# Norms after the attention projection and after `down`: squares of two neighbouring chunks added on POOL, one ones-product per pair

## What is computed

```python
def rms_norm(x, g):
    xf = x.astype(jnp.float32)
    y = xf * lax.rsqrt(jnp.mean(xf * xf, axis=-1, keepdims=True) + RMS_EPS)
    return (y * g.astype(jnp.float32)).astype(x.dtype)

hp = modulate(rms_norm(xp, norm_g[l, 0]), sh1c, sc1c)
xp = xp + g1c * yp                                  # yp: attention @ w_o, or convolution @ w_pw2
hp = modulate(rms_norm(xp, norm_g[l, 1]), sh2c, sc2c)
xp = xp + g2c * (jnp.square(jax.nn.relu(hp @ w_up)) @ w_down)
```

## Time and profile before

| | us |
|---|---|
| three runs: median (lowest, highest) | 2685.6 (2671.91, 2939.64) |
| the profiled execution, its own time | 2670.14 |
| its span, slowest core (core 0) | 2668.6 |
| spans of the eight cores | 2657.3 to 2668.6 |
| mean granted TensorE clock of core 0 | 0.968 |

### The profile page before, as it was taken

How to read it: one execution, slowest core, us unless ns; L and a number is a source line. 1 busy time by engine, 2 the same in 40 slices (tenths; PEclk the granted TensorE clock), 3 DMA queues, 4 the chain that set the end, 5 groups by cost and what they waited for, 6 DMA issues and landing times.

```text
span 2668.6 us, 41955 instructions; the slowest of 8 cores (2657.3 to 2668.6 us)
## 1 busy us (share of the span) xinstructions
PE 2445.8 (92%) x14955; PEld 1077.7 (40%) x15184; DVE 1107.2 (41%) x1552; ACT 1051.0 (39%) x1563; POOL 336.8 (13%) x395
## 2 busy tenths in 40 slices
PE   2888889999999988999999888899999998899998
PEld 1322224444444443444443222344444454344443
DVE  1344444422325565323244554443232555632333
ACT  3455555301224466202254555551031445730224
POOL 1122220000001141000002322000000112200000
PEclk8999989999999989999999999899999998999999
DMA  9765533455543212555438444156664331233432
GB/s 208 149 87 69 71 57 62 78 99 100 99 76 68 54 29 48 102 101 98 79 73 155 56 56 56 20 76 101 99 101 72 61 60 31 32 48 50 55 54 95
DMA packets 133434, 205.99 MB, mean 77 GB/s; under 512 B 73136, under 2 KB 79280, under 8 KB 132464
## 3 DMA queue, kind: packets, MB, share of 16 engines
q0 software_dynamic: 109872, 161.70, 41.4%
q1 hardware_dynamic: 23360, 41.60, 4.7%
HBM read 322.89 MB, written 31.46 MB: 133 GB/s over the span
## 4 chain that ended last, share of the span: by engine, by line
PE 77%; DMA 6%; ACT 6%; issue 5%; DVE 5%; POOL 1%; DVEq 0%; ACTq 0%; POOLq 0%; SPq 0%
PE pp L654 23%; PE ps L654 19%; PE pp L677 7%; PE ps L884 4%; PE pp L1276 3%; DMA scr<-rpbp 3%; PE pp L1003 2%; PE ps L677 2%; PE pp L1404 2%; PE ps L1028 2%; PE ps L1276 2%; PE pp L1239 2%; PE ps L582 2%; DMA ring<-wall 2%; DVE scr L976 1%
## 5 line engine op out<-in xcount | busy, mean ns | idle before, releaser
L723 DVE TENSOR_TENSOR big<-big 128x512 bf16<-128x512 f32 x384 | 265.5, 692 | 415.8 <-ACT big L721 415.8
L654 PE MATMUL ps<-hTs,ring 128*128 128x512 bf16 x1488 | 339.0, 383 | 13.5 <-ACT hTs L632 8.5
L654 PE MATMUL pp<-hTs,ring 128*128 128x512 bf16 x1520 | 342.7, 380 | 1.9
L419 POOL DMA_DIRECT2D ring<-wall x140 | 99.1, 708 | 1712.7 <-PE pp L654 492.9
L654 PE MATMUL pp<-big,ring 128*128 128x512 bf16 x1362 | 304.9, 379 | 2.8 <-ACT big L721 1.2
L721 ACT ACTIVATE big<-ps 128x512 f32<-128x512 f32 x190 | 113.2, 596 | 472.5 <-PE ps L654 468.2
L575 ACT ACTIVATE scr<-xTs 128x512 bf16<-128x512 f32 x216 | 133.3, 626 | 318.8 <-DVE xTs L693 277.0
L693 DVE SCALAR_TENSOR_TENSOR xTs<-pp,mod,xTs 128x512 f32<-128x512 f32 x156 | 116.8, 750 | 330.2 <-PE pp L654 239.4
L976 DVE TENSOR_TENSOR scr<-pp,scr 128x768 f32<-128x768 f32 (+2 forms) x192 | 174.5, 910 | 143.1 <-PE pp L1009 69.3
L721 ACT ACTIVATE big<-pp 128x512 f32<-128x512 f32 x194 | 115.4, 596 | 296.7 <-PE pp L654 293.8
L654 PEld LDWEIGHTS ps<-hTs,ring 128*128 128x128 bf16 x1520 | 148.6, 98 | 192.3 <-issue 18.7
(11 more groups left out here) (120 smaller groups left out, 2689.8 us busy)
## 6 DMA issues: line engine op xcount, KB each, us to landing
ring<-wall POOLq DMA_DIRECT2D x140, 1024.0 KB, 11.2
vo<-big SPq DMA_DIRECT2D x48, 256.0 KB, 5.6
kTo<-big SPq DMA_DIRECT2D x48, 256.0 KB, 2.1
scr<-rpbp POOLq DMA_DIRECT2D x64, 128.0 KB, 3.6
xTs<-xT SPq DMA_DIRECT2D x3, 2048.0 KB, 19.8
yT<-scr SPq DMA_DIRECT2D x24, 256.0 KB, 2.2
scr<-big SPq DMA_DIRECT2D x64, 54.0 KB, 6.8
scr<-big POOLq DMA_DIRECT2D x64, 54.0 KB, 6.8
```

Of the source, the lines that this page charges most:

```text
L654: ins = e.matmul(ps[pi][:, :], lhsT=w[:, kc, fc * fw:(fc + 1) * fw], rhs=src[:, kc, t * 512:(t + 1) * 512], start=(kc == 0), stop=(kc == n ...
L723: P.op("dve", lambda e: e.tensor_tensor(out=hid[:, hc, t * 512:(t + 1) * 512], in0=ta[:, :], in1=ta[:, :], op=ALU.mult), reads=[ta_r], wri ...
```

## The change

`norm_begin` takes `pair`. With it, `norm_chunk` squares into an fp32 buffer of 128x512; for an even chunk it stops there. For an odd chunk POOL adds the two squares into a bf16 buffer, and the ones-product of this sum is deferred, with the lag that the odd chunk had. A tile has four ones-products instead of eight. It is set for the norm behind `o` and for the norm behind `down` if another layer follows; the final norm, the first one and those behind the convolution stay as they are.

```diff
+        ctx["np"] = 4 if pair else 8
+        ctx["sq"] = [scr.alloc(1024, BF16, f"sq{n}") for n in range(4 if pair else 6)]
+        if pair:
+            ctx["sqf"] = [scr.alloc(2048, F32, f"sqf{n}") for n in range(4)]
+            ctx["qf"] = 0
...
+        if ctx["np"] == 4:
+            sf, sf_r = ctx["sqf"][ctx["qf"] % 4]
+            ctx["qf"] += 1
+            P.op("act", lambda e: e.activation(out=sf[:, :], in_=xT[:, t, c, :], func=AF.Square),
+                 reads=[xT_r[c][t]], writes=[sf_r])
+            if c % 2 == 0:
+                ctx["half"] = (sf, sf_r, c, t)
+                return
+            s0, s0_r, c0, t0 = ctx["half"]
+            assert (c0, t0) == (c - 1, t)
+            sq, sq_r = ctx["sq"][ctx["q"] % 4]
+            ctx["q"] += 1
+            P.op("pool", lambda e: e.tensor_tensor(out=sq[:, :], in0=s0[:, :], in1=sf[:, :], op=ALU.add),
+                 reads=[s0_r, sf_r], writes=[sq_r])
...
-                                          start=(n == 0), stop=(n == 7)),
+                                          start=(n == 0), stop=(n == ctx["np"] - 1)),
...
-            if n == 7:
+            if n == ctx["np"] - 1:
...
-                nctx = norm_begin("mod", l + 1, 0) if l + 1 < DEPTH else norm_begin("final")
+                nctx = norm_begin("mod", l + 1, 0, pair=True) if l + 1 < DEPTH else norm_begin("final")
...
-        nctx = norm_begin("mod", l, 1)
+        nctx = norm_begin("mod", l, 1, pair=True)
```

More of the change, by code:

```diff
@@ L550, in build_program, with norm_begin @@
     ntiles = []
-    def norm_begin(kind, l=None, k=None, banks=(5, 6, 7)):
+    def norm_begin(kind, l=None, k=None, banks=(5, 6, 7), pair=False):
         flush_deferred()
@@ L555, in norm_begin @@
         ctx = {"kind": kind, "l": l, "k": k, "n": 0, "m": 0, "q": 0, "cnt": [0] * NT}
-        ctx["sq"] = [scr.alloc(1024, BF16, f"sq{n}") for n in range(6)]
+        ctx["np"] = 4 if pair else 8
[3 more added lines that the diff above has]
+            ctx["qf"] = 0
         ctx["rstd"] = [scr.alloc(2048, F32, f"rstd{n}") for n in range(2)]
@@ L572, in norm_chunk @@
         bk = ctx["bk"][t]
[L573 to L577, removed]
+        if ctx["np"] == 4:
[12 more added lines that the diff above has]
+                 reads=[s0_r, sf_r], writes=[sq_r])
+        else:
+            sq, sq_r = ctx["sq"][ctx["q"] % 6]
+            ctx["q"] += 1
+            P.op("act", lambda e: e.activation(out=sq[:, :], in_=xT[:, t, c, :],
+                                               func=AF.Square),
+                 reads=[xT_r[c][t]], writes=[sq_r])
         def part():
```

## The result

The changed kernel takes 1.0089 times the time before (95% interval 1.0059 to 1.0119), about 24 us more. In three of its five executions one die ran at a lower clock, so this goes by the other two, 2694.2 and 2699.0 us, and not by the median of 2744.19 us. Timed once more beside the experiments it took 1.0065 (1.0036 to 1.0093), about 17 us more. The forecast was 5 us more, 2676 us, with a range to 2697.

The account below looks back on a forecast made before the run. PE, busy for 92% of the span, was taken to bound the kernel. 13.0 us saved and 18.2 lost gave +5.2 on a profiled 2670.1, about 2675; it predicted 2676 us, range 2657 to 2697.

Parts of the forecast that it names:

- The price of the addition: On POOL, adding two fp32 128x512 tiles into bf16: 1.27 us taken, with bounds of 0.61 and 1.89.
- the places of the large stalls: PE waits for late sums: 2.03 us at product 11 of `o`; in `down` 0.9 at 17 and 21, 1.57 at 23.
- The saving of 13.0: On PE, five norms lose 12 ones-products each: 60 x 0.2165 = 13.0 us, 0.5% of the span.
- The rival of a slow addition: On POOL, the addition with bf16 output takes 1.89 us and nearly every pair stalls: 2703 us, chance 0.12.
- The rival that all is hidden: In the five norms, late products find unseen slack and all 13.0 us are kept: 2657 us, chance of this side 0.12.
- POOL's queue: Behind `o` and `down`, weight loads wait for the last sums; counted as hidden, uncovered up to 4 us at each of five places.
- A rival for late loads: At five places the loads become late behind the sums: 5 x 4 = 20 us, giving 2695 us, chance 0.05.
- 18.2: Microseconds PE was to lose in 17 places behind `o` and `down`, waiting for sums from POOL.
- small waits that were there before the change: In `o`, eight groups and eight products took 15.77 us instead of 15.56: a stall of 0.2 for each tile, which goes.
- +5.2: Net microseconds over five norms: +1.4 for each of two behind `o`, +0.8 for each of three behind `down`.
- the hand-overs: From square to product, ACT to POOL takes 0.15 us and POOL to PE 0.14; with the addition 1.56.

Follow-up runs that it names:

- early loads: The changed kernel with the two weight loads at the end of `o` and `down` put on POOL's queue ahead of the last additions; 1.0036 of the time before.

## Why the forecast was right about the stalls and wrong about the loads

**Right.** The price of the addition (1.265 against 1.27) and the places of the large stalls: products 11 and 19 of `o`, 17, 21 and 23 of `down`. By the list of waits they are 2.08 and 0.91 against 2.03 and 0.9. The saving of 13.0 is confirmed where the stalls are gone (2.4 and 2.6 for a norm). The rival of a slow addition falls: bf16 output costs nothing. The rival that all is hidden falls as well. The answer to which engine mattered is the one given: POOL is 15% busy, and its latency of 1.6 us in an in-order chain outweighs 13 us of PE's work.

**The step that failed** is "POOL's queue", where the loads were called hidden. It asked only whether a piece arrives before PE uses it, and that holds behind `o` and `down`. (PE's one wait for the ring in `down` of layer 0, 3.0 us on core 0 before and 5.6 on core 2 after, varies from core to core in both kernels: the stage takes 89 to 95 us before and 91 to 95 after, median 92.5 and 92.9.) It didn't ask what else the DMA engines do in that time, nor what stands behind the load on the same queue. The rows that say so were in the trace of before: a share of 0.97 in the stretch, and `gtab` waiting 11.75 for its own landing behind two weight loads. A rival for late loads was there, with 20 us at five places; it is one place, with 5 to 6 us.

**Mis-sized terms.** That 18.1 meets 18.2 is in part luck. The forecast counted a stall from the place at which PE would have issued the product, 0.22 behind the matmul before it, and took off 0.8 for small waits that were there before the change. The list of waits counts from the end of the recorded 0.38 of the matmul before. The starts of the products tell the loss as the forecast meant it. The changed kernel, core 0, first `o` in layer 0, then `down` in layer 1:

```profile
428.46 0.38 PE L601 MATMUL ps<-scr,onesb 128*128 128x512 bf16 x1
...
434.30 0.38 PE L601 MATMUL ps<-scr,onesb 128*128 128x512 bf16 x1 [2.01 <-POOL scr L589]
...
438.16 0.38 PE L601 MATMUL ps<-scr,onesb 128*128 128x512 bf16 x1
```
```profile
1365.42 0.38 PE L601 MATMUL ps<-scr,onesb 128*128 128x512 bf16 x1 [0.83 <-POOL scr L589]
...
1372.54 0.38 PE L601 MATMUL ps<-scr,onesb 128*128 128x512 bf16 x1
...
1380.73 0.38 PE L601 MATMUL ps<-scr,onesb 128*128 128x512 bf16 x1 [0.90 <-POOL scr L589]
...
1387.81 0.38 PE L601 MATMUL ps<-scr,onesb 128*128 128x512 bf16 x1 [1.52 <-POOL scr L589]
```

Steady products of `o` are 3.67 apart. Product 11 comes after 5.84 and product 13 after 3.86: 2.17 and 0.19 late (forecast 2.03 and 0.18), and products 19 and 21 the same. In `down` the steady distance is 7.12; products 17, 21 and 23 are 1.0, 1.07 and 1.69 late (forecast 0.9, 0.9 and 1.57; one of the two groups before product 23 has 8 matmuls, so 5.39 is due there). That is 4.8 for each norm behind `o`, less 0.5 for waits of before (0.21 and 0.28 on core 0 in layer 2; the forecast had 0.4), and 3.8 for each behind `down`: some 20 us instead of 18.2, and +7 us instead of +5.2 with the saving taken off. One part of it is in the second profile above: the hand-overs measured 0.26 and 0.15 at product 11, 1.68 in all and not 1.56. Between squares 0 and 23 of `o`, where 11 products (2.4) are gone, this gives 4.8 - 0.5 - 2.4 = 1.9, as the stages have it in layer 2; 1.6 had been worked out.

With early loads the stages, as medians, are still 9.7 us over before, not 7. A wait of PE that the kernel before doesn't have is one part: in the changed kernel the first product of `up` in layer 2 comes 0.9 late (an idle 0.74, which the list puts down to the last gated addition of `o`, line 712), on all eight cores. The stage between the last square of `o` and the first of `down` is 266.6 or 268.3 there, and 265.7 or 267.4 before. The two values in each kernel are the clock. The same 16 matmuls in the kernel before, on core 0 (267.4) and core 3 (265.8):

```profile
1764.08 5.30 PE L654 MATMUL ps<-hTs,ring 128*128 128x512 bf16 x16 [2.84 <-ACT hTs L632]
```
```profile
1766.13 3.61 PE L654 MATMUL ps<-hTs,ring 128*128 128x512 bf16 x16 [2.86 <-ACT hTs L632]
```

Both stand behind a wait of 2.8. On core 0 the granted clock from 1765.3 to 1768.7 is 0.50 of full speed (1.2 GHz), on core 3 it is 1.00 in the same place: 1.7 us. Three cores of eight have the low stretch there before the change, four after it. A stall that the change itself makes does this too, in `o` of layer 2 behind the 2.0 us of product 11, on cores 0 and 1 (core 0, then core 3):

```profile
1737.72 4.50 PE L696 MATMUL pp<-big,ring 128*128 128x512 bf16 x13
```
```profile
1750.38 2.97 PE L696 MATMUL pp<-big,ring 128*128 128x512 bf16 x13
```

`o` takes 47.9 and 48.0 on these two cores and 46.4 on the other six. So a stall can cost 1.5 us more than its wait; in the repetition no core shows it at this place, and why one core falls and another doesn't stays open. What is left of the 9.7, some 2 us, lies in the number of cores with a low stretch (0.8 in the stage behind `o`), behind the last square (0.4 to 0.7) and in stages that scatter as much. Of the first 24 us, the means of the stages account for 17, and the repetition has no more; 16.6 of the 28.8 us between the profiled spans arose on core 2 ahead of every changed instruction.

## What to carry to other kernels

To move work off a busy in-order engine, compare not the loads but the time at which the moved result is due: walk from the producer through every hand-over to the consumer's place in its queue, most of all where the producers are behind. Then look at what else the new engine's queue issues, and read the DMA share of the stretch that a delayed load runs into: in a stretch at 0.97, as here, a load that is put off takes from others, whatever the date of its own use. Change the lag together with the work; here the same edit is 0.7 to 0.9% slower with the old lags and load order and 0.27% faster with new ones.

## What the runs showed of the hardware

- The GpSimd addition of two fp32 tiles of 128x512 takes 1.265 us with bf16 output and 1.27 with fp32 output. The GPSIMD Engine Reference of the Trainium skill (Elementwise, side-by-side cycle accounting) puts a two-input operation at about 2.6 cycles for each element, an estimate of 1.11 us without dispatch; the trace has 1.27.
- POOL waited 11.75 us for a small DMA behind two loads of 128x4096 on the same queue when the first of them had a head start, and 20.32 when both were issued just ahead of it.
- A change of ACT's table costs 1.28 us, and moving Ln past one sigmoid brought two of them in each layer.
- Behind a wait of TensorE of 2.0 us (two cores of eight) and of 2.8 us (three of eight, in the stage behind `o`) the granted clock stood at 0.50 of full speed, 1.2 GHz instead of 2.4, for the next 3.4 us; 16 matmuls of 128x512 then took 5.30 us instead of 3.61.
